# A two-block transformer kernel on one NeuronCore: weight tiles laid at eight distances from a 128-byte line, activation pages half a line on

## The reference, cut to what matters

```
h = layer_norm(ALPHA * x + 0.5 * swiglu(x, ffn1_w_gu, ffn1_w_down))
proj = h @ w_in
merged = sum(gates * einsum('bsnc,ncd->bsnd', branches, w_branch))
h = layer_norm(ALPHA * h + merged @ w_out)
h = layer_norm(ALPHA * h + 0.5 * swiglu(h, ffn2_w_gu, ffn2_w_down))
...
hdn = xn @ w_up
out = (gelu(g) * u) @ w_down
```

## Time and profile before

| | |
|---|---|
| median of 3 runs | 3524.08 us (3522.23 to 3526.37) |
| the profiled execution | 3520.0 us |
| its span (first to last instruction) | 3518.2 us |
| PE busy | 3457.2 us, 98% |
| PEld busy (weight loads) | 2940.1 us, 84% |
| DVE busy | 2226.0 us, 63% |
| ACT busy | 1681.5 us, 48% |
| DMA | 102 GB/s on average, main queue 30.1% of the 16 engines' time |

### The profile page before, as it was taken

How to read it: one execution, slowest core, us unless ns; L and a number is a source line. 1 busy time by engine, 2 the same in 40 slices (tenths; PEclk the granted TensorE clock), 3 DMA queues, 4 the chain that set the end, 5 groups by cost and what they waited for, 6 DMA issues and landing times.

```text
span 3518.2 us, 49763 instructions
## 1 busy us (share of the span) xinstructions
PE 3457.2 (98%) x19256; PEld 2940.1 (84%) x19256; DVE 2226.0 (63%) x4229; ACT 1681.5 (48%) x3243; POOL 111.5 (3%) x132
## 2 busy tenths in 40 slices
PE   9999999999999999999999999999999999999999
PEld 7998888877889998999888877888977677788887
DVE  5566666556775667566665566774666787666643
ACT  5355455554354545444555543553546443444432
POOL 0010000000000100010000000000100000000000
PEclk9999999999999999999999999999999999999999
DMA  5475331112335743474221112255622222233332
GB/s 156 133 173 145 119 96 46 49 46 67 96 101 139 171 126 99 135 174 129 90 70 45 52 58 87 87 147 138 160 89 89 61 70 86 75 95 97 96 97 89
DMA packets 198276, 358.86 MB, mean 102 GB/s; under 512 B 22102, under 2 KB 26359, under 8 KB 198040
## 3 DMA queue, kind: packets, MB, share of 16 engines
q1 hardware_dynamic: 178840, 321.32, 30.1%
q0 software_dynamic: 18432, 33.56, 5.7%
q10 hardware_dynamic: 768, 0.79, 0.1%
HBM read 350.60 MB, written 4.72 MB: 101 GB/s over the span
## 4 chain that ended last, share of the span: by engine, by line
PE 91%; DVE 5%; ACT 3%; issue 1%; DMA 0%; DVEq 0%; SPq 0%; ACTq 0%
PE bank L2492 21%; PE bank L2501 21%; PE bank L2493 20%; PE bank L2527 6%; PE bank L2530 6%; PE bank L2529 6%; PE bank L2480 2%; PE bank L2475 1%; PE bank L2570 1%; PE bank L2663 1%; DVE w_lo L3237 1%; PE bank L2673 1%; PE bank L2538 1%; DVE page_r L3279 1%; PE bank L2590 1%
## 5 line engine op out<-in xcount | busy, mean ns | idle before, releaser
L2492 PE MATMUL bank<-page_r,w_hi 128*128 128x512 f32 (+1 forms) x3446 | 1367.9, 397 | 25.4 <-DVE w_lo L3237 17.9
L2501 PE MATMUL bank<-page_r,w_lo 128*128 128x512 f32 (+1 forms) x3446 | 1343.4, 390 | 0.0
L2493 PE MATMUL bank<-page_r,w_hi 128*128 128x512 f32 (+1 forms) x3446 | 1332.1, 387 | 0.0
L2492 PEld LDWEIGHTS bank<-page_r,w_hi 128*128 128x128 f32 x3446 | 650.2, 189 | 170.1 <-DVE w_lo L3237 22.9
L2815 ACT ACTIVATE w_hi<-raw 128x512 fp32r<-128x512 f32 x864 | 532.5, 626 | 532.0 <-PE bank L2501 523.2
L2501 PEld LDWEIGHTS bank<-page_r,w_lo 128*128 128x128 f32 x3446 | 649.3, 188 | 129.5
L2493 PEld LDWEIGHTS bank<-page_r,w_hi 128*128 128x128 f32 x3446 | 650.5, 189 | 125.2 <-issue 3.6
L3237 DVE TENSOR_TENSOR w_lo<-raw,w_hi 128x512 fp32r<-128x512 f32 x864 | 574.4, 686 | 143.8 <-ACT w_hi L2815 141.7
L2527 PE MATMUL bank<-page_r,w_hi 128*128 128x256 f32 x1792 | 507.3, 283 | 2.4 <-DVE w_lo L3255 2.4
L2529 PE MATMUL bank<-page_r,w_hi 128*128 128x256 f32 x1792 | 507.1, 283 | 0.0
L2530 PE MATMUL bank<-page_r,w_lo 128*128 128x256 f32 x1792 | 507.1, 283 | 0.0
(11 more groups left out here) (322 smaller groups left out, 3457.2 us busy)
## 6 DMA issues: line engine op xcount, KB each, us to landing
raw<-weights SPq DMA_DIRECT2D x864, 256.0 KB, 2.6
raw<-pairs SPq DMA_DIRECT2D x320, 256.0 KB, 3.3
raw<-pairs POOLq DMA_DIRECT2D x128, 256.0 KB, 5.8
page_f<-x_t SPq DMA_DIRECT2D x8, 256.0 KB, 5.0
bias_rows<-page_f SPq DMA_DIRECT2D x8, 256.0 KB, 2.0
page_f<-bias_rows SPq DMA_DIRECT2D x8, 256.0 KB, 3.8
out_t<-page_f SPq DMA_DIRECT2D x12, 128.0 KB, 1.8
cst<-consts SPq DMA_DIRECT2D x4, 272.0 KB, 3.6
```

What stands on the lines that cost most here:

```text
L2492: self.e.matmul(o, hi, X.hi[kt], start=first, stop=False)
L2493: self.e.matmul(o, hi, X.lo[kt], start=False, stop=False)
L2501: last = self.e.matmul(o, lo, X.hi[kt], start=False, stop=final)
```

## The change

Every unit of `raw` and `w_hi` becomes 544 columns wide (`PITCH`, 2176 bytes, 17 lines of 128 bytes), of which 512 are used. Where in its unit a slab lies is set by `slab_phase`: 0, 4, 8, ... 28 columns, that is 0, 16, 32, ... 112 bytes past a line of 128, the next one every 36 slabs, so that the 864 slabs pass through the eight distances three times. Pairs take the next distance every 8 pairs, once through in all. The rounded copy of a slab has the distance of its raw one. A unit lent as a page lies at distance 0. The instructions that work on two units at once (L2824, L3255) now have two runs of 512 columns with 32 between them instead of one run of 1024.

To make room `small` shrinks from 2048 to 1184 columns; `line_end` grows to 24. From `cst` to the first page there are now 16,832 bytes, which is 64 more than a multiple of 128: all pages start half a line on. `mean_rounded` stays 96 bytes past a line. No instruction is added or removed, and the order of all engines is the same.

```diff
-LINE_END = 8
+LINE_END = 24
+SMALL = 1184
+PHASES = (0, 4, 8, 12, 16, 20, 24, 28)
 UNIT = SLAB * P
+PITCH = UNIT + 32
...
+def slab_phase(s):
+    return PHASES[s // 36 % len(PHASES)]
+
+def pair_phase(n):
+    return PHASES[n // 8 % len(PHASES)]
...
     def __init__(self, region, rounded, at, landed, added=None):
-        super().__init__(region[:, at * UNIT:(at + 1) * UNIT], rounded[:, at * UNIT:(at + 1) * UNIT])
+        super().__init__(None)
         self.at, self.region, self.rounded, self.landed, self.loads = at, region, rounded, landed, 0
         self.added, self.adds = added, 0
+        self.place(0)
+
+    def place(self, phase):
+        self.phase, a = phase, self.at * PITCH + phase
+        self.f, self.r = self.region[:, a:a + UNIT], self.rounded[:, a:a + UNIT]
+        return self
+
+    def two(self, region):
+        both = region[:, self.at * PITCH:(self.at + 2) * PITCH].rearrange("p (u c) -> p u c", u=2)
+        return both[:, :, self.phase:self.phase + UNIT]
 
     def wide(self):
-        return self.region[:, self.at * UNIT:(self.at + 2) * UNIT]
+        return self.two(self.region)
...
-            slot = lender.take()
+            slot = lender.take().place(0)
...
-        self.raw = sb("raw", [P, NRAW * UNIT])
+        self.raw = sb("raw", [P, NRAW * PITCH])
...
-        self.w_hi = sb("w_hi", [P, NHI * UNIT], F32R)
+        self.w_hi = sb("w_hi", [P, NHI * PITCH], F32R)
...
-        self.small = sb("small", [P, 2048])
+        self.small = sb("small", [P, SMALL])
...
-            unit = self.raws.take()
+            unit = self.raws.take().place(slab_phase(self.next_raw))
...
-        out = s1, s3 = self.raws.take_pair()
+        phase = pair_phase(p.number)
+        out = s1, s3 = [x.place(phase) for x in self.raws.take_pair()]
```

More of the change, by code:

```diff
@@ L156, in __init__ @@
     def __init__(self, region, rounded, at, landed, added=None):
-        super().__init__(region[:, at * UNIT:(at + 1) * UNIT], rounded[:, at * UNIT:(at + 1) * UNIT])
+        super().__init__(None)
         self.at, self.region, self.rounded, self.landed, self.loads = at, region, rounded, landed, 0
         self.added, self.adds = added, 0
+        self.place(0)
[6 more added lines that the diff above has]
+        return both[:, :, self.phase:self.phase + UNIT]
     def wide(self):
-        return self.region[:, self.at * UNIT:(self.at + 2) * UNIT]
+        return self.two(self.region)
     def wide_rounded(self):
-        return self.rounded[:, self.at * UNIT:(self.at + 2) * UNIT]
+        return self.two(self.rounded)
 class Stock:
@@ L443, in __init__ @@
         self.table, self.buckets, self.out = table, buckets, out
-        with nc.sbuf_tensor("w_lo", [P, NRAW * UNIT], F32R) as lo:
+        with nc.sbuf_tensor("w_lo", [P, NRAW * PITCH], F32R) as lo:
             self.w_lo = lo
-        self.raw = sb("raw", [P, NRAW * UNIT])
-        with nc.sbuf_tensor("w_lent", [P, NHI * UNIT], F32) as lent:
+        self.raw = sb("raw", [P, NRAW * PITCH])
+        with nc.sbuf_tensor("w_lent", [P, NHI * PITCH], F32) as lent:
             self.w_lent = lent
-        self.w_hi = sb("w_hi", [P, NHI * UNIT], F32R)
+        self.w_hi = sb("w_hi", [P, NHI * PITCH], F32R)
         self.cst = sb("cst", [P, NCONST])
@@ L536, in small @@
         self.small_at += n
-        assert a + n <= 2048
+        assert a + n <= SMALL
         return self.m.small[:, a:a + n]
@@ L561, in rounded @@
             self.loaded(self.next_round)
-            raw, hi = self.slab[self.next_round] = [self.slab[self.next_round][0], self.his.take()]
+            raw, hi = self.slab[self.next_round] = [self.slab[self.next_round][0],
+                                                     self.his.take().place(slab_phase(self.next_round))]
             self.round_slab(self.next_round, raw, hi)
@@ L915, in prepare @@
         add("a11", s3)
-        a11 = self.raws.take()
+        a11 = self.raws.take().place(phase)
         load("a11", a11)
         yield
-        a12, a22 = self.raws.take_pair()
+        a12, a22 = [x.place(phase) for x in self.raws.take_pair()]
         load("a12", a12)
@@ L922, in prepare @@
         yield
-        s2, s4 = self.raws.take_pair()
+        s2, s4 = [x.place(phase) for x in self.raws.take_pair()]
         k.will(vector="second")
         self.sum_second(p, s1, a11, s2)
-        h11 = self.his.take()
+        h11 = self.his.take().place(phase)
         k.will(scalar="h11")
@@ L931, in prepare @@
         yield
-        h13 = self.his.take_pair()
+        h13 = [x.place(phase) for x in self.his.take_pair()]
         k.will(scalar="h13")
@@ L939, in prepare @@
         self.rest_units(p, out, h13, k["h13"])
-        h24 = self.his.take_pair()
+        h24 = [x.place(phase) for x in self.his.take_pair()]
         k.will(scalar="h24")
@@ L945, in prepare @@
         yield
-        h12, h22 = self.his.take_pair()
+        h12, h22 = [x.place(phase) for x in self.his.take_pair()]
         k.will(scalar="h12")
```

## The result

The changed kernel takes 3543.85 us (median of 4 runs, 3539.88 to 3545.89) against 3523.73 us of the kernel before, run beside it: a ratio of 1.0055, 95% interval 1.0038 to 1.0072. The forecast was 96 us more; the runs show some 20. The profiled span grew from 3518.2 to 3538.1 us.

What follows compares the result with a forecast made beforehand. TensorE's matmuls were taken to bound the kernel. 3520.0 us plus 96 us for weights off the line, all else 0, gave 3616, or 3620 us as the median of runs; range 3465 to 3735 us.

Steps and rivals of the forecast that it cites:

- What bounds the kernel: TensorE, busy 98% of the span and 91% of the chain of waits; other engines' work mostly covered.
- Part (1): Slab and pair weights: 13,750 of 15,714 loads start off a line of 128 bytes, 7 ns each, 96 us.
- one isolated load: L2544, weights 96 bytes past a line: its load costs 5 + 7 = 12 ns, spread on two gaps.
- Part (2): Streamed operands in pages half a line on: bounds 0 and 189 us, taken as 0 in the sum.
- What would show it: Tests in trace windows: gaps stepping with distance; raised alike at distance 0 and 64 would blame pages, not weights.
- Parts (3) to (7): Wide instructions in two runs, VectorE and ScalarE off line, slab loads, plain float32 matmuls, resized `small` and `line_end`: nothing counted.
- The rule of the Trainium skill: TensorE has two independent read ports and never waits; lines are 16 bytes: 3520 us and no more.
- gain rival: Weights and pages both on a line collide; other distances save 11.5 ns per fast matmul, 3456 us at three of eight; 22%.
- heavy rival: Every weight load off the line pays 12 ns: 165 us more, 3689 us; 18%.
- The picture of a collision with the weight load: In fast matmuls, the weight load's reads collide with the streamed operand's, giving some 11.5 ns overhead that addresses can change.

Runs made afterwards that it cites:

- everything off the line: Kernel before with 64 bytes of padding ahead of everything, so weights and pages both start 64 past a line: 3524.03 us, 1.0002.
- without the levelling: Kernel with slabs meant for difference 0, pairs 64 bytes past and pages on a line, but slabs at the start of their unit: 3518.45 us, 0.9990.
- 16/0: Stream of 48 matmuls alone, computation left out, weights 16 bytes past a multiple of 256 and operand at 0: 226.7 ns, or 233.3 after stream 112/0 (weights 112, operand 0).

## Why the prediction was right and wrong

**What bounds the kernel: right.** PE is 92% of the chain and takes all of the difference, 21.5 us more busy time on a span 19.9 us longer; its idle time before the first matmul of a block stayed at 24 us (25 before).

**Part (1), weights off the line: the step that failed.** It took "off a line of 128 bytes" as what costs, 12 ns from one isolated load, and made 7 ns on 13,750 loads of it, 96 us. The trace after has 3.2 ns on 10,338 slab matmuls (33.0 us) and -2.8 ns on 5376 pair matmuls (-15 us). Three things are in that. The criterion was wrong: what counts first is the difference of the two starts modulo 256 bytes, as the kernel with everything off the line (no cost) and the one without the levelling (slabs and pages on lines, but odd and even units mixed, 4 ns on each slab matmul in its last window) show. The sign differs with the width, which neither the sum nor the range saw: 256 columns have their worst place, or near it, at difference 0 and their best at 64 and 192. And an isolated load does not price a run of loads: a stream settles again, at 16/0 on the very 226.7 ns. The 12 ns themselves were read rightly (the starts give 235 and 231 to 232 ns, 13 together). That the sign came out as forecast is partly luck: it is the balance of a loss and a gain, and with all weights at distance 0 the same layout costs nothing (0.9998).

**Part (2), pages: 0 was wrong in substance.** The prediction had bounds of 0 and 189 us. Moved alone, the pages gave 8 us back, which is below the lower bound, 5 ns less on each pair matmul and 1 to 3 more on a slab one. And the change had a part that the prediction did not list: units 2176 bytes apart change the difference from unit to unit by an odd line, which costs 32 us on slabs whose distance is 0 (3518.45 us without the levelling, 3486.34 with it). For the same reason slabs were slower in the stretch at 64 too (231.5 ns), which by the prediction's "What would show it" would have put the cost on the pages; with the pages back on a line the kernel was no faster (3547.92 us).

**Parts (3) to (7): right.** 1218 and 1056 ns for the wide instructions in two runs, 685 and 626 for the others, landing 2.7 us. TensorE waits for them about as long as before: 15.3 us for L3261 and 2.6 for L3279, against 17.9 and 2.4. The plain float32 matmuls kept their records of 592 ns (L2611, L2635 after).

**The rivals.** The rule of the Trainium skill that TensorE never waits on anyone and that lines are 16 bytes ("SBUF — State Buffer", "Who interferes with whom" and "Specifications (TRN2)") would have given 3524 us; the measured 20 us more, and 37 us less with each width at its own difference, disagree. It fits the bfloat16 streams, which show 2.5 ns at each of the four distances tried. The gain rival, at 22%, had the mechanism that the pairs show: the old distance was their bad one. It was given for all fast matmuls, and for slabs it is the reverse: at 512 columns none of the distances tried beat the old one. The heavy rival (12 ns on every load, 239 ns) found no support: no float32r stream of 512 columns at full clock exceeded 236.7 ns.

**What is open.** The picture of a collision with the weight load, from which the prediction argued, is not borne out for slabs: with a quarter of the load the time above the columns is 18.3 ns, not less than 13.3, and it grows with the streamed operand. For pairs it is neither shown nor excluded: there a smaller load does take away the same 6.7 ns as a better difference, and a full load fills nearly the whole matmul. Plain float32 and bfloat16 don't show the time, but they also differ in how fast they stream or how long they load, so which property matters is not shown. That the starts matter, with a period of 256 bytes, that the difference accounts for most but not all of it, and that a stream can settle on different gaps at the same starts, is shown; by what mechanism was not found.

## What to carry to other kernels

In a kernel bound by matmuls of the rounded type (float32r), measure the gap from start to start in a window of one kind, and compare it with bfloat16's 2.5 ns over the columns: what is above may depend on where weights and streamed operand start relative to each other modulo 256 bytes. Measure it by width before moving anything: the same 64 bytes took 6.7 ns from 256 columns and added 6.7 to 512. Choose each width's difference by itself and keep it from buffer to buffer; with a distance between buffers that is not a multiple of 256 bytes, slabs lost 32 of the 37 us gained here. A table of streams is a guide and no more: the same difference with other starts, or after another stream, gave up to 6.7 ns more or less, so the whole kernel has to be measured. And one odd instruction in a settled stream is no price for a stream of such instructions.

## What the runs showed of the hardware

- float32r matmuls of 512 columns with full weight loads took 226.7 to 236.7 ns and those of 256 columns 113.3 to 122.3 ns, with nothing but addresses and the stream before changed and the clock at its full level; bfloat16 took 215.8 and 109.2 at each of four distances.
- A full float32r weight load (128 columns) takes 111.7 ns by itself, one of 96 columns 85.0: the gaps of streams of 128 columns. In bfloat16 the same stream took 55.8.
- The period is 256 bytes: from a difference of 0, shifts of one operand by 256, 512 and 1024 bytes changed nothing, a shift of the rest of the weights by 128 took 226.7 to 231.1 ns.
- The settled gap depends on the stream before: 226.7 or 233.3 ns for weights at 16 and operand at 0.
- VectorE and ScalarE showed no dependence on the eight distances: over all 864 slabs L3261 took 674 to 696 ns and L2839 612 to 700, before 674 to 696 and 612 to 701.
